# The operand buffer of a two-block transformer kernel, placed 32 bytes higher in SBUF

## The chip, the cores and the metric

The kernel runs on one core of one Trainium2 chip. The metric is the device time of one execution in microseconds (us); the kernel before took 1439.92 us as the median of 3 runs.

## The reference, cut to what matters

Two transformer blocks run one after the other on 256 tokens of width 1024, in float32. Nearly all of the work is products of normalised activations with weight matrices:

```python
def conformer_conv(h, ...):  # h @ w_pw1, gate, 31-tap convolution, layernorm, silu, @ w_pw2
def fox_attention(h, w_q, w_o, k, v, c_bhs): ...      # 16 heads
def memory_cross_attention(h, mem_n, ...): ...        # 4 heads, twice
def sqrelu_mlp(h, w1, w2):
    return jnp.square(jax.nn.relu(h @ w1)) @ w2       # 1024 -> 4096 -> 1024, twice
def swiglu(x, w_gate, w_up, w_down):
    return (jax.nn.silu(x @ w_gate) * (x @ w_up)) @ w_down   # 1024 -> 2816 -> 1024, twice
def token_mixing(u, w_in, ...):                       # u @ w_in (5136 columns), two attentions, @ w_out
...
u = modulate(rmsnorm_2(h, norm_ff1[l]), sh1, sc1)     # mod = silu(c) @ w_ada + b_ada
```

## The kernel before, in words

**Tiles.** Activations lie transposed: 128 partitions hold 128 features, KT = 8 such tiles make up the width, and the T = 256 tokens run along the free axis. Most products are made in "split" form. A tensor is kept as a high part, rounded to the type that TensorE reads in one pass (fp32r), and a low part that holds the rest. ScalarE writes the high part and VectorE the low part, for weights (`wsplit`, lines 1176 and 1753) as for activations.

**Buffers.** `hA` is the operand buffer of the normalised tiles: per feature tile 2 x 256 elements, the high block and then the low block. `hM`, `hB` and `hid` have the same layout. `hM` and `hB` hold the operands of the output projections (`hB` also a second normalised operand), `hid` the hidden activations of the four feed-forward parts; they and others share one 64 KB region behind the fixed buffers. `raw` receives weights by DMA, 1 MB a chunk in a ring of 4; `wsplit` is the ring of split weights.

**The two inner forms.** A pair (`block_cols`, lines 477 and 479) multiplies one 128 x 128 weight tile with both blocks of the operand at once (512 columns) and then the low weights with the high block (256 columns):

```python
        def tile_of(hl):
            return lambda kt: hl[:, kt, :].rearrange("p (s t) -> p s t", s=2)
        def block_cols(dst, w, lo_w, h, start, stop):
            nc.tensor.matmul(dst.rearrange("p (s t) -> p s t", s=2), w, h, ...)         # L477
            return nc.tensor.matmul(dst[:, 0:T], lo_w, h[:, 0, :], ...)                 # L479
```

In a pair the weights are the stationary operand, loaded ahead of each matmul (the rows of PEld), and the activations stream. A triple does the same as three matmuls of 256 columns: lines 536 to 538 (`whole_tile`, used for the last tiles of a residual and for the branch products), and 565 to 568 in the output projection of the first attention. In lines 516 to 518 (`split_values`, the values of the second memory attention), and in the pairs 636 and 640 (products that give rows: the value projections and part of the input projection), it is the other way round: `hA` is stationary and `wsplit` streams. Line 498 multiplies unsplit float32 tiles, some of them from `pw1_h`, which lies where `hA` lies.

**Order.** The stages follow one another on all engines by semaphores: pw1 and the memory projections in unsplit form (to about 155 us), memv1, pw2, memq0, memo0, up0, down0, the first attention, memq1, memo1, up1, down1, gu1, dn1, the input projections with the second attentions, branch, out, gu2, dn2. `hA` streams in memq, up, gu, the key projections of the first attention and most of the input projections; `hid` in down and dn. Beside this VectorE makes the modulation vector from `w_ada` in steps of 256 KB (line 2142, buffer `ada_w`, loaded on SP's queue), at listed chunks of down0, the first attention, down1, gu1, dn1, the input projections and gu2.

**Placement.** One function hands out bytes of a partition from a running cursor:

```python
        cursor = [-(-nc.sbuf_base // 32) * 32]
        def place(name, shape, dt=F32, at=None):
            size = int(np.prod(shape[1:])) * (2 if dt == BF16 else 4)
            if at is None:
                at = cursor[0]
                cursor[0] += -(-size // 32) * 32
            return nc.alloc_sbuf_tensor_at(name, shape, dt, offset=at)
```

Of the kernel before, what the change touches and what calls it, by code (L numbers as in the profile page):

```python
# [236 lines left out]
def program(nc, dram, out):  # L237
    ctx = ExitStack()
    with ctx:
# [9 lines that stand above are left out]
# [2 lines left out]
        wsplit = place("wsplit", [P, RING, 2, KT * 256], F32R)  # L251
        x = place("x", [P, KT, T])

        rel_rows = place("rel_rows", [P, G_HEADS, SKEW], at=cursor[0])
        hA_at = cursor[0]
        hA = place("hA", [P, KT, 2 * T], F32R)
        tsum = place("tsum", [P, 2, 2, T])
        aux = place("aux", [P, 2, 2, T])
        lowp = place("lowp", [P, 2, T])
# [2455 lines left out]
```

How the kernel before makes its waits and increments, by code:

```python
        @block.sync  # L401
# [5 lines left out]
            def load(st, c, known):  # L407
                slot = (st.base + known) % RING
                n = st.ring + known - RING
                if n >= 0:
                    prev = next(s for s in PLAN if s.ring <= n < s.ring + s.chunks)
                    sp.wait_ge(S("native_done" if prev.native else "w_lo"), c + (st.ring - RING - prev.ring + prev.base + 1))
                sp.dma_start(raw[:, slot, 0:st.elems], dram[st.name][c]).then_inc(raw_loaded[slot], 16)
# [12 lines left out]
            def ada_load(m):  # L427
                for half in range(2):
                    if m:
                        sp.wait_ge(S("ada_step"), 2 * (m - 1) + half + 1)
                    else:
                        sp.wait_ge(S("cond_silu"), 1)
                    sp.dma_start(ada_w[:, half, :], dram["ada"][m, half]).then_inc(ada_loaded[half], 16)
# [11 lines left out]
                    continue  # L446
                groups(sp, st.chunks, lambda c, known: load(st, c, known), begun=RING if st.ring == 0 else 0,
                       lead=RING if st.ring == 0 else 0)
            for p in range(PAIRS):
                sp.wait_ge(S("final_ready"), p + 1)
                sp.dma_start(out[:, 2 * p:2 * p + 2, :], x[:, 2 * p:2 * p + 2, :]).then_inc(S("stored"), 16)
            sp.wait_ge(S("stored"), 16 * PAIRS)
# [4 lines left out]
            def weights_ready(st, c):  # L458
                pe.wait_ge(S("w_hi"), c + (st.base + 1))
                pe.wait_ge(S("w_lo"), c + (st.base + 1))
```

## Time and profile before

| | us |
|---|---|
| median of 3 runs | 1439.92 |
| the 3 runs | 1438.95, 1439.92, 1442.92 |
| span of the profiled execution, first to last instruction | 1437.8 |
| TensorE matmuls busy | 1411.5 (98%) |
| VectorE busy | 1111.5 (77%) |
| ScalarE busy | 690.4 (48%) |
| DMA | 279.31 MB, mean 194 GB/s |

The profiled execution is given by its span; what a run takes beyond it is 2.1 us by the median. The profile has a time of its own only as that span. A busy TensorE is not yet a TensorE at full rate, since matmuls are pipelined and their ends are modelled: how fast it works is read from the distance between the starts of consecutive matmuls in the timeline. The chain of waits then tells in which stretches TensorE's rate sets the end, and in which another engine does.

### The profile page before, as it was taken

The page shows a single profiled execution, that of the slowest core. Times are in us where ns is not written, and L with a number is a line of the kernel's source. Part 1 is how long each engine was busy: PE and PEld are TensorE (multiplying, and loading weights), DVE is VectorE, ACT ScalarE, POOL GpSimd, SP SyncE. Part 2 cuts the span into 40 slices and gives each one's busy share as a digit, 9 for nine tenths or more (in the row PEclk, how much of TensorE's full clock was granted, in tenths as well). Part 3 has the DMA queues.
Part 4 walks back from the last instruction along what each step waited for, and adds up shares of the span by engine and source line. Part 5 has one row for each costly group of instructions (what it writes and reads, how often), then busy time and mean ns, then how long its engine had stood idle before and what let it go on. Part 6 is the DMA issues. An engine that isn't in the chain of part 4 may idle for free.

```text
span 1437.8 us, 21872 instructions
## 1 busy us (share of the span) xinstructions
PE 1411.5 (98%) x8580; PEld 1243.6 (86%) x8580; DVE 1111.5 (77%) x1660; ACT 690.4 (48%) x899; POOL 33.1 (2%) x21
## 2 busy tenths in 40 slices
PE   7999999999999999999999999999999999999997
PEld 6878998888889888888888988888988889888887
DVE  3799876698767887758887779997578678798664
ACT  2221664455434654645563355553454447555442
POOL 0000000000000000000000000000024100000000
PEclk9999999999999999999999999999999999999999
DMA  7444663355686456525558747757553436475451
GB/s 265 144 167 153 251 214 123 118 186 208 236 292 207 169 188 219 183 94 182 191 204 279 268 179 273 272 188 260 203 204 135 169 103 226 159 273 205 135 179 66
DMA packets 60150, 279.31 MB, mean 194 GB/s; under 512 B 6590, under 2 KB 8063, under 8 KB 35232
## 3 DMA queue, kind: packets, MB, share of 16 engines
q1 hardware_dynamic: 56248, 270.69, 53.7%
q10 hardware_dynamic: 3816, 7.45, 1.5%
q8 instruction: 58, 0.95, 0.3%
q14 instruction: 28, 0.23, 0.0%
HBM read 273.89 MB, written 4.19 MB: 193 GB/s over the span
## 4 chain that ended last, share of the span: by engine, by line
PE 84%; DVE 8%; DMA 5%; ACT 1%; issue 1%; DVEq 0%; SPq 0%; ACTq 0%
PE acc L477 34%; PE acc L479 17%; PE acc L498 10%; DMA ada_w<-in_ada 5%; PE acc L536 3%; PE acc L538 3%; PE acc L537 3%; DVE wsplit L1753 2%; PE acc L636 2%; PE stat L721 2%; DVE ada_w L2142 2%; PE acc L640 1%; PE turned L741 1%; PE stat L833 1%; PE score L1054 1%
## 5 line engine op out<-in xcount | busy, mean ns | idle before, releaser
L477 PE MATMUL acc<-hA,wsplit 128*128 128x512 f32 x1664 | 589.9, 399 | 4.4 <-DVE tsum L1767 1.7
L1176 ACT ACTIVATE wsplit<-raw 128x2048 fp32r<-128x2048 f32 (+3 forms) x214 | 381.2, 1783 | 195.3 <-PE acc L479 145.1
L1753 DVE TENSOR_TENSOR wsplit<-raw,wsplit 128x2048 fp32r<-128x2048 f32 (+3 forms) x214 | 455.1, 2130 | 16.4 <-ACT wsplit L1176 16.4
L479 PE MATMUL acc<-hA,wsplit 128*128 128x256 f32 x1664 | 463.9, 279 | 0.0
L477 PEld LDWEIGHTS acc<-hA,wsplit 128*128 128x128 f32 x1664 | 312.3, 188 | 81.6 <-issue 4.1
L479 PEld LDWEIGHTS acc<-hA,wsplit 128*128 128x128 f32 x1664 | 313.4, 188 | 0.4
L477 PE MATMUL acc<-hid,wsplit 128*128 128x512 f32 x648 | 224.9, 390 | 0.0
L479 PE MATMUL acc<-hid,wsplit 128*128 128x256 f32 x648 | 182.7, 282 | 0.0
L1186 ACT ACTIVATE lowp<-acc 128x512 f32<-128x512 f32 (+1 forms) x118 | 69.0, 585 | 202.8 <-PE acc L479 174.9
L477 PEld LDWEIGHTS acc<-hid,wsplit 128*128 128x128 f32 x648 | 121.6, 188 | 25.6
L479 PEld LDWEIGHTS acc<-hid,wsplit 128*128 128x128 f32 x648 | 122.5, 189 | 0.0
L2178 DVE SCALAR_TENSOR_TENSOR conv<-upad,taps,conv 128x256 f32<-128x256 f32 x240 | 98.2, 474 | 0.8
L2142 DVE CUSTOM_DVE_ANT_0 ada_w<-ada_w,cact,cols 128x512 f32<-128x512 f32 x72 | 55.0, 763 | 39.7 <-DMA ada_w<-in_ada 38.9
L2142 DVE CUSTOM_DVE_ANT_0 ada_w<-ada_w,cact,mod 128x512 f32<-128x512 f32 x72 | 54.9, 762 | 14.3 <-DMA ada_w<-in_ada 4.4
L536 PE MATMUL acc<-hid,wsplit 128*128 128x256 f32 x216 | 61.0, 282 | 0.0
L537 PE MATMUL acc<-hid,wsplit 128*128 128x256 f32 x216 | 60.3, 279 | 0.0
L538 PE MATMUL acc<-hid,wsplit 128*128 128x256 f32 x216 | 60.3, 279 | 0.0
L1763 DVE TENSOR_TENSOR tsum<-acc,lowp 128x512 f32<-128x512 f32 x40 | 27.6, 690 | 39.3 <-ACT lowp L1186 39.1
L498 PE MATMUL acc<-mem_h,raw 128*128 128x256 f32 x256 | 56.5, 380 | 0.0
L498 PEld LDWEIGHTS acc<-mem_h,raw 128*128 128x128 f32 x256 | 48.4, 190 | 8.7 <-issue 2.3
L498 PE MATMUL acc<-pw_h,raw 128*128 128x256 f32 x256 | 55.7, 379 | 0.0
L498 PEld LDWEIGHTS acc<-pw_h,raw 128*128 128x128 f32 x256 | 48.6, 190 | 6.6
(315 smaller groups left out, 2051.6 us busy)
## 6 DMA issues: line engine op xcount, KB each, us to landing
raw<-in_gu SPq DMA_DIRECT2D x44, 1024.0 KB, 4.9
ada_w<-in_ada SPq DMA_DIRECT2D x144, 256.0 KB, 4.8
raw<-in_up SPq DMA_DIRECT2D x32, 1024.0 KB, 4.9
raw<-in_down SPq DMA_DIRECT2D x32, 1024.0 KB, 5.0
raw<-in_dn SPq DMA_DIRECT2D x32, 704.0 KB, 4.1
raw<-in_pw SPq DMA_DIRECT2D x12, 1024.0 KB, 8.1
raw<-in_memk SPq DMA_DIRECT2D x8, 1024.0 KB, 4.8
raw<-in_memv SPq DMA_DIRECT2D x8, 1024.0 KB, 5.3
```

Of the source, the lines that this page charges most:

```text
L477: nc.tensor.matmul(dst.rearrange("p (s t) -> p s t", s=2), w, h, start=start, stop=False, skip_group_check=True)
L479: return nc.tensor.matmul(dst[:, 0:T], lo_w, h[:, 0, :], start=False, stop=stop, skip_group_check=True)
L498: mm = nc.tensor.matmul(acc[:, par, j, 0:T], lhs, rhs, start=kt == 0, stop=kt == KT - 1)
L536: nc.tensor.matmul(dst, w, h[:, 0, :], start=start, stop=False, skip_group_check=True)
L537: nc.tensor.matmul(dst, w, h[:, 1, :], start=False, stop=False, skip_group_check=True)
L538: return nc.tensor.matmul(dst, lo_w, h[:, 0, :], start=False, stop=stop, skip_group_check=True)
L636: nc.tensor.matmul(dst.rearrange("p (s n) -> p s n", s=2), h(kt)[:, 0, tt * P:(tt + 1) * P], w[:, :, kt * n:(kt + 1) * n], start=kt == 0, ...
L1176: nc.scalar.activation(wsplit[:, slot, 0, 0:elems_of(n)], raw[:, slot, 0:elems_of(n)], ACT.Copy).then_inc(S("w_hi"), 1)
L1186: last = nc.scalar.activation(lowp[:, :, 0:width], acc[:, par, :, width:2 * width], ACT.Copy)
L1753: V.tensor_tensor(wsplit[:, slot, 1, 0:e], raw[:, slot, 0:e], wsplit[:, slot, 0, 0:e].bitcast(F32), ALU.subtract).then_inc(S("w_lo"), 1)
L2142: V.tensor_tensor_reduce(w, w, cact[:, half * HALF:(half + 1) * HALF], 1.0, mod[:, m:m + 1] if half else col("ada_b", m), ALU.mult, ALU.ad ...
L2178: ins = V.scalar_tensor_tensor(out=conv[:, kt, :], in0=u, scalar=w, in1=conv[:, kt, :], op0=ALU.mult, op1=ALU.add)
```

## The change

The cursor is moved by 32 bytes ahead of `hA`, and by another 32 bytes behind it.

```diff
         x = place("x", [P, KT, T])
 
+        cursor[0] += 32
         rel_rows = place("rel_rows", [P, G_HEADS, SKEW], at=cursor[0])
         hA_at = cursor[0]
         hA = place("hA", [P, KT, 2 * T], F32R)
+        cursor[0] += 32
         tsum = place("tsum", [P, 2, 2, T])
```

All engines issue the same instructions in the same order on the same shapes. What differs is the byte offset of operands in their partition, as the built program has them:

| buffer | before | after | remainder by 64 | remainder by 128 | remainder by 256 |
|---|---|---|---|---|---|
| `raw` | 16512 | 16512 | 0 | 0 | 128 |
| `wsplit` | 49280 | 49280 | 0 | 0 | 128 |
| `x` | 114816 | 114816 | 0 | 0 | 128 |
| `hA`, `pw1_h`, `gain_sq`, `rel_rows` | 123008 | 123040 | 0, then 32 | 0, then 32 | 128, then 160 |
| `tsum` (and `aux`, `lowp`, `rstd`, `var`, `cols`, `mod`) | 139392 | 139456 | 0 | 0, then 64 | 128, then 192 |
| `ada_w` (and `cact`, `ones`, the masks, `small`) | 159648 | 159712 | 32 | 32, then 96 | 160, then 224 |
| `hid`, `hM`, `hB` | 163744 | 163808 | 32 | 32, then 96 | 160, then 224 |
| `fo`, `gl` | 204704 | 204768 | 32 | 32, then 96 | 160, then 224 |
| `mo` | 180128 | 180192 | 32 | 32, then 96 | 160, then 224 |

The tiles inside `hA`, `hM`, `hB` and `hid` lie 2048 bytes apart, the weight tiles inside `wsplit` 512 bytes, so that every tile has its buffer's remainder.

## Rows read from the trace of the kernel before

**Rows 1.** The page: busy time, the granted clock in 40 slices, the chain by engine.
```profile
PE 1411.5 (98%) x8580; PEld 1243.6 (86%) x8580; DVE 1111.5 (77%) x1660; ACT 690.4 (48%) x899; POOL 33.1 (2%) x21
...
PEclk9999999999999999999999999999999999999999
...
PE 84%; DVE 8%; DMA 5%; ACT 1%; issue 1%; DVEq 0%; SPq 0%; ACTq 0%
```
**Rows 2.** Groups of PE, by form: line, tiles, shape, count | busy us, mean ns | idle.
```profile
L477 PE MATMUL acc<-hA,wsplit 128*128 128x512 f32 x1664 | 589.9, 399 | 4.4 <-DVE tsum L1767 1.7 <-DVE x L1838 1.2 <-DVE hA L1969 0.8
L479 PE MATMUL acc<-hA,wsplit 128*128 128x256 f32 x1664 | 463.9, 279 | 0.0
L477 PE MATMUL acc<-hid,wsplit 128*128 128x512 f32 x648 | 224.9, 390 | 0.0
L479 PE MATMUL acc<-hid,wsplit 128*128 128x256 f32 x648 | 182.7, 282 | 0.0
...
L477 PE MATMUL acc<-hM,wsplit 128*128 128x512 f32 x144 | 50.5, 393 | 0.0
```
**Rows 3.** Timeline of PE in dn2, `hid`: start us, length; first and last of 28 L477.
```profile
1389.63 0.39 PE L477 MATMUL acc<-hid,wsplit 128*128 128x512 f32 x1
...
1398.99 0.39 PE L477 MATMUL acc<-hid,wsplit 128*128 128x512 f32 x1
```
**Rows 4.** Timeline of PE in gu2, `hA`: first and last of 26 L477.
```profile
1309.86 0.40 PE L477 MATMUL acc<-hA,wsplit 128*128 128x512 f32 x1
...
1318.69 0.40 PE L477 MATMUL acc<-hA,wsplit 128*128 128x512 f32 x1
```
**Rows 5.** Timeline of PE in up0, `hA`: first and last of 27 L477.
```profile
299.66 0.39 PE L477 MATMUL acc<-hA,wsplit 128*128 128x512 f32 x1
...
308.68 0.39 PE L477 MATMUL acc<-hA,wsplit 128*128 128x512 f32 x1
```
**Rows 6.** Chain of waits in gu1: start us, us, what.
```profile
849.31 0.69 DVE tsum L1767
...
852.90 4.88 DMA ada_w<-in_ada
...
948.14 0.50 PE acc L477
```
**Rows 7.** Chain of waits in gu2.
```profile
1249.91 0.61 ACT lowp L1186
...
1254.19 4.93 DMA ada_w<-in_ada
...
1298.09 0.51 PE acc L477
```
**Rows 8.** Timeline of PE in the input projections, `hA`: first and last of 10 L477.
```profile
1073.90 0.40 PE L477 MATMUL acc<-hA,wsplit 128*128 128x512 f32 x1
...
1077.09 0.40 PE L477 MATMUL acc<-hA,wsplit 128*128 128x512 f32 x1
```
**Rows 9.** Timeline of PE in memv1, `hA` stationary: first and last of 18 L516.
```profile
171.74 0.28 PE L516 MATMUL acc<-wsplit,hA 128*128 128x256 f32 x1
...
177.86 0.28 PE L516 MATMUL acc<-wsplit,hA 128*128 128x256 f32 x1
```
**Rows 10.** Timeline of PE in down0, triples of `hid`: first and last of 21 L536.
```profile
445.92 0.28 PE L536 MATMUL acc<-hid,wsplit 128*128 128x256 f32 x1
...
452.92 0.28 PE L536 MATMUL acc<-hid,wsplit 128*128 128x256 f32 x1
```
**Rows 11.** Timeline of PE, row products, `hA` stationary: first and last of 14 L636.
```profile
1096.61 0.40 PE L636 MATMUL acc<-wsplit,hA 128*128 128x512 f32 x1
...
1101.20 0.40 PE L636 MATMUL acc<-wsplit,hA 128*128 128x512 f32 x1
```
**Rows 12.** Groups of DVE, by form: the low block written into `hA` and into `hB`.
```profile
L1824 DVE TENSOR_TENSOR hA<-tsum,hA 128x512 fp32r<-128x512 f32 x13 | 8.9, 686 | 3.2 <-ACT hA L1260 3.2
...
L1982 DVE TENSOR_TENSOR hB<-tsum,hB 128x512 fp32r<-128x512 f32 x4 | 2.7, 687 | 0.1
```
**Rows 13.** Timeline of PE behind down0, bf16 matmuls of 256 columns.
```profile
457.76 4.09 PE L741 MATMUL turned<-mask_bf,ident_bf 128*128 128x256 bf16 x36
```

## The prediction

> **What bounds the kernel now.** First the page's busy times, the clock and the chain [rows 1]: TensorE is busy 98% of the span, the granted clock shows 9 in all 40 slices (its upper level, 2.4 GHz, throughout), and 84% of the chain is PE. So the end is set, for the most part, by how fast TensorE works through its matmuls. No instruction moves, so no wait is added or removed by the program. The only thing that can change is how long an access to SBUF takes at another address. The question is thus whether any duration in the trace depends on the place of an operand.
>
> Next the groups by form [rows 2]. The same line 477, on the same shape and with the same weights buffer, has a mean of 399 ns where `hA` streams and 390 ns where `hid` streams; line 479 has 279 against 282. Matmul ends are modelled, so I go to the starts in the timeline. In dn2, where `hid` streams, 28 starts of L477 span 1398.99 - 1389.63 = 9.36 us, that is 27 periods of 346.7 ns [rows 3]. In gu2, where `hA` streams, 26 starts span 8.83 us, 25 periods of 353.2 ns [rows 4]. A pair with `hA` is there 6.5 ns longer. But `hA` isn't always slower: in up0 27 starts span 9.02 us, 26 periods of 346.9 ns [rows 5].
>
> Counted from start to start over the whole trace, all pairs of `hid`, `hM` and `hB` that wait for nothing keep one period of about 346.7 ns, from the third pair after any wait on. Pairs of `hA` fall into one of several repeating patterns, of 347, 353 or 360 ns, keep it for many chunks, and leave it at a stall. The only property that separates the two kinds of buffer and that the change touches is the address: `hA` begins at a multiple of 64 (as `wsplit` does), the others 32 bytes past one. After the change `hA` has the remainder that `hid` had, by 64, by 128 and by 256. I read the rows so: which patterns exist depends on the phase between the stream and the weights, and at 32 there is one alone, the fast one.
>
> **The change, part by part.** *The operand streams from its new place (pairs).* I price each stage by its own surplus over 346.7 ns, and count it only where the chain runs through PE.
> - up0, up1 and the first part of gu1: no surplus [rows 5], nothing to gain.
> - gu1 up to 948.14: from 849.31 to there the chain is VectorE's in-order queue and the loads of `ada_w`, such as the 4.88 us at 852.90 [rows 6]. A faster TensorE only waits longer for it, so the surplus of some 0.6 us late in this stretch goes into that wait. Behind it 3 of the 22 chunks are left: 48 pairs x 6.5 ns = 0.3 us.
> - gu2: from 1249.91 to 1298.09 the chain is again VectorE and `ada_w` [rows 7]; 136 pairs x 6.5 ns = 0.9 us would be lost in the wait at its end. Before it 24 pairs give 0.15 us; behind it 12 chunks, 192 pairs x 6.5 ns = 1.25 us.
> - Input projections: 256 pairs of `hA`, chunks between 347 and 354 ns; the chunk shown has 3.19 us for 9 periods, 354.4 ns [rows 8]. I take half of that surplus, 3.5 ns, for all: 0.9 us. The 64 pairs of the key projections likewise: 0.2 us.
> - memq0, memq1: steady pairs at 347, nothing.
>
> Sum: 0.3 + 0.15 + 1.25 + 0.9 + 0.2 = 2.8 us.
>
> *The operand is stationary.* In memv1 `hA` is loaded as weights: 18 starts of L516 span 6.12 us, 360.0 ns a triple [rows 9], while a triple of `hid` takes 7.00 us / 20 = 350.0 ns [rows 10]. For 64 triples that is 0.6 us. The row products have 4.59 us / 13 = 353.1 ns in the chunk shown [rows 11]; half of that surplus over 128 pairs is 0.4 us. No row shows a stationary operand at 32 beside a stream at 0, so this is bounded by 0 and 1.0 us; I take half, 0.5 us, since it is the same two streams with their roles exchanged.
>
> *Branch.* 64 triples of `gl`, `mo` and `hA` follow one another there, so that the pattern of one may carry into the next; bounded by 0 and 64 x 10 ns = 0.6 us; I take 0.3.
>
> *Everything else.* VectorE's writes into the buffer: 686 ns at 0, 687 ns at 32 in `hB` [rows 12], so nothing. The buffers behind keep their remainder by 64; I price them at nothing and put the doubt into a rival.
>
> Sum: 2.8 + 0.5 + 0.3 = **3.6 us less**. The span of 1437.8 us becomes 1434.2, and with the 2.1 us that the median has above that span the forecast is 1439.9 - 3.6 = **1436.3 us**. The bounds of the priced terms are 2.8 and 4.4 us; if the chain misleads in gu1 and gu2 and TensorE's surplus counts there too, another 1.5: 5.9 us, 1434.0.
>
> **The rivals.** *The place doesn't matter: 1439.9 us.* For it: `hA` reached 346.9 ns at its old place in up0 [rows 5], so the place alone doesn't make it slow; `hA` differs from `hid` also by lying some 40 KB lower, and a pattern could come from where the last stall fell. Against it: `hid`, `hM` and `hB` start anew many times, also straight after `hA`, and always end in the same period.
>
> The Trainium skill speaks for this rival. Its page "SBUF — State Buffer", section "SBUF: two separate sides", has it that TensorE and ScalarE have ports of their own and never wait for anyone. Its page "TensorE: Matmul & The Clock Gate", section "Step-by-step: what each phase is for", gives the stream and the weights independent read ports. And that page's section "Back-to-back issue gap" has N / 2.4 + 2.5 ns between warm matmuls, 215.8 + 109.2 = 325 ns for a pair, wherever it lies. By these rules the change would be worth 0. The bf16 matmuls of 256 columns agree, with 36 of them in 4.09 us [rows 13]; the pairs don't, since 346.7 is above 325, and 353.2 beside 346.7 on one shape isn't foreseen.
>
> *Slower: the buffers behind leave their good phase.* `hid`, `hM`, `hB` and `fo` go from remainder 32 to 96 by 128. If the pattern repeats at 128 bytes (or 256) and not at 64, then `hA` gains as above, but 904 pairs that now have one fast pattern could fall into one like that of gu2: 904 x 6.5 ns = 5.9 us, and their 344 triples into that of memv1: 344 x 10 ns = 3.4 us. down and dn lie on TensorE's part of the chain, so it counts in full: 1436.3 + 9.3 = 1445.6 us. It decides where the period is above 64. Nothing in the trace excludes it, since all tiles that stream in pairs lie at 0 or 32 by 128; for a shorter period speaks only that the smaller step is the simpler reading. *The same mechanism with the other sign*: at 96 the pairs could also find a shorter pattern than any seen; with the same size, 5.9 us, the time would be 1430.4.
>
> That the change doesn't do what it says is excluded: the built program has the new offsets.
>
> **How the numbers follow.** A measurement of this kernel can tell about 0.3%, 4.3 us, from no change: faster is below 1435.6, slower above 1444.2. Chances: forecast 0.61, no effect of the place 0.24, slower 0.09, the shorter pattern 0.06. The forecast's own spread (1434.0 to 1437.1, and about 1 us of scatter between medians) puts a third of its chance below 1435.6: 0.21, with the last case 0.27; slower 0.10, of which a little is scatter; the rest, 0.63, within 0.3%. The range for 8 in 10 goes from 1433.6, just below the strongest form of the forecast, to 1441.8, the no-change case with the scatter that the runs before show above their median; it leaves out most of the slower case and the shorter pattern.
>
> **What would show it.** Right: in gu2 the starts of L477 are 346.7 ns apart, and L477 and L479 of `hA` have means near 390 and 282 ns; memv1's triples are at 350; the waits ahead of 948 and 1298 us grow by about 0.6 and 0.9 us, with the loads of `ada_w` in the chain as before; down and dn keep 346.7. Wrong: gu2 still at 353 (the place doesn't matter), or `hid` at 353 or 360 (the period is above 64). If `hA`'s pairs are all at 346.7 but the span shrinks by less than 2.8 us, the step on the chain is at fault.

## The result, and the profile after

The changed kernel takes 1443.85 us (median of 12 runs, 1442.94 to 1444.49), the kernel before 1439.74 us in the runs beside it (1438.95 to 1442.92): ratio 1.0024, 95% interval 1.0017 to 1.0031. It is 4.1 us **slower**. I forecast 3.6 us less, so the sign was wrong, and the time lies above my range.

The page of the changed kernel, busy times and the chain by engine (lines below L256 carry numbers higher by 2 than before, so L477 is now L479):

```profile
PE 1415.1 (98%) x8580; PEld 1250.2 (87%) x8580; DVE 1111.4 (77%) x1660; ACT 690.4 (48%) x899; POOL 33.2 (2%) x21
...
PE 84%; DVE 8%; DMA 5%; ACT 1%; issue 1%; DVEq 0%; SPq 0%; ACTq 0%
```

Nothing has moved between engines: same shares as in [rows 1]. So the periods have to tell. First gu2, where `hA` streams, first and last of 27 starts of L479 in the timeline of PE:

```profile
1308.65 0.39 PE L479 MATMUL acc<-hA,wsplit 128*128 128x512 f32 x1
...
1317.67 0.39 PE L479 MATMUL acc<-hA,wsplit 128*128 128x512 f32 x1
```

9.02 us for 26 periods: 346.9 ns, where [rows 4] had 353.2. That is as forecast. (The views give starts to 0.01 us, so a period read over 26 of them is good to about 0.4 ns: 346.5, 346.7 and 346.9 are the same.) Then dn2, where `hid` streams, first and last of 27 starts:

```profile
1393.85 0.39 PE L479 MATMUL acc<-hid,wsplit 128*128 128x512 f32 x1
...
1402.95 0.39 PE L479 MATMUL acc<-hid,wsplit 128*128 128x512 f32 x1
```

9.10 us for 26 periods: 350.0 ns, where [rows 3] had 346.7. This buffer moved by 64 bytes, and I had priced that at nothing. The triples of `hid` in down0, first and last of 23 starts of L538 (L536 before):

```profile
446.72 0.28 PE L538 MATMUL acc<-hid,wsplit 128*128 128x256 f32 x1
...
454.64 0.28 PE L538 MATMUL acc<-hid,wsplit 128*128 128x256 f32 x1
```

7.92 us for 22 periods: 360.0 ns, where [rows 10] had 350.0. And memv1, `hA` stationary, first and last of 18 starts of L518 (L516 before):

```profile
171.81 0.28 PE L518 MATMUL acc<-wsplit,hA 128*128 128x256 f32 x1
...
177.85 0.28 PE L518 MATMUL acc<-wsplit,hA 128*128 128x256 f32 x1
```

6.04 us / 17 = 355.3 ns, where [rows 9] had 360.0: half of the possible gain, which would have ended at 350.0.

**A ledger.** The two kernels issue the same 8580 matmuls in the same order, so each start of one can be set against the same start of the other. The difference grows or shrinks stage by stage; added up over the traces:

| stages | what streams | change, us |
|---|---|---|
| start, up to pw1 | `aux` | +0.9 |
| down0, down1, dn1, dn2 | `hid` | +4.3 |
| pw2, memo0, memo1, outputs of the first attention | `hM`, `hB`, `fo` | +1.4 |
| branch, out | `gl`, `mo`, `hA`, then `hM` | +0.5 |
| memv1, memq, gu1, input projections, gu2 | mostly `hA` | -2.6 |
| end | | +4.5 |

The mean durations are treacherous here. For `hid` they were 390 and 282 ns in [rows 2] and are now:

```profile
L479 PE MATMUL acc<-hid,wsplit 128*128 128x512 f32 x648 | 227.1, 393 | 0.0
L481 PE MATMUL acc<-hid,wsplit 128*128 128x256 f32 x648 | 180.9, 279 | 0.0
```

393 + 279 is the same sum as 390 + 282, although the period of the pair grew by 3.3 ns. Ends of matmuls are modelled in the profile; only the starts showed it.

The 0.9 us at the start can't be put down to the change. The first matmul of pw1 begins at 13.37 us in the profile of before, at 14.27 in the one after, and between 13.56 and 14.60 in the profiles of the eight kernels below, with a different number of the first statistics matmuls (L721, 16 of them) 426 ns apart and most of the others 216. Before has the earliest of the ten. Without this start the spans of the two profiles differ by 3.6 us. There is one profile for each kernel, so whether the start scatters from run to run of one kernel isn't shown; the medians include it.

### The profile page after: what moved, and what is told of

Same layout as the page of the kernel before. It is cut to its first block, busy times and chain, and to the rows that moved or that the text cites. A ratio compares the mean times of both kernels' runs of the same rounds, so it can differ in the third digit from the quotient of the medians.

```text
span 1442.4 us, 21872 instructions
## 1 busy us (share of the span) xinstructions
PE 1415.1 (98%) x8580; PEld 1250.2 (87%) x8580; DVE 1111.4 (77%) x1660; ACT 690.4 (48%) x899; POOL 33.2 (2%) x21
## 4 chain that ended last, share of the span: by engine, by line
PE 84%; DVE 8%; DMA 5%; ACT 1%; issue 1%; DVEq 0%; SPq 0%; ACTq 0%
PE acc L479 34%; PE acc L481 17%; PE acc L500 10%; DMA ada_w<-in_ada 5%; PE acc L538 3%; PE acc L540 3%; PE acc L539 3%; DVE wsplit L1755 2%; PE acc L638 2%; PE stat L723 2%; DVE ada_w L2144 2%; PE acc L642 1%; PE turned L743 1%; PE stat L835 1%; PE score L1056 1%
## 5 line engine op out<-in xcount | busy, mean ns | idle before, releaser
L479 PE MATMUL acc<-hA,wsplit 128*128 128x512 f32 x1664 | 585.9, 394 | 5.1 <-DVE tsum L1769 2.4
L481 PE MATMUL acc<-hA,wsplit 128*128 128x256 f32 x1664 | 469.0, 282 | 0.0
L479 PEld LDWEIGHTS acc<-hA,wsplit 128*128 128x128 f32 x1664 | 312.4, 188 | 74.7 <-DVE tsum L1769 4.6
L479 PE MATMUL acc<-hid,wsplit 128*128 128x512 f32 x648 | 227.1, 393 | 0.0
L479 PEld LDWEIGHTS acc<-hid,wsplit 128*128 128x128 f32 x648 | 121.4, 187 | 29.1
L538 PE MATMUL acc<-hid,wsplit 128*128 128x256 f32 x216 | 61.8, 286 | 0.0
```

Source lines behind the costliest of these rows:

```text
L481: return nc.tensor.matmul(dst[:, 0:T], lo_w, h[:, 0, :], start=False, stop=stop, skip_group_check=True)
L538: nc.tensor.matmul(dst, w, h[:, 0, :], start=start, stop=False, skip_group_check=True)
```

## The experiments

Three theories stood against each other. **A**: what counts is the phase of the streamed operand against the stationary one (for a pair, the distance from `wsplit`), and it repeats not before 128 bytes. **B**: the absolute place of the streamed operand counts. **C**: the loss comes from `hA`, or from the small buffers between. All remainders below are by 128.

### Only hA moves

```diff
+        mod = place("mod", [P, N_MOD * KT])
         rel_rows = place("rel_rows", [P, G_HEADS, SKEW], at=cursor[0])
...
-        mod = place("mod", [P, N_MOD * KT])
```

> Only hA moves to remainder 32 (by 64, 128 and 256): mod, 288 bytes, is placed ahead of hA in place of behind it, so hid, hM, hB, fo, ada_w and ones keep their old offsets; tsum, aux, lowp, rstd, var and cols go from 0 to 32. Theory A (the phase of the streamed operand against the weights, repeating at 128 bytes: 32 good, 0 mixed, 96 bad): pairs of hA at 346.8 ns, pairs of hid stay at 346.7, triples of hid at 350.0, memv1's triples near 355; the time is that of before less the 2.1 us that the changed kernel won in memv1, gu1, gu2 and the projections, 1437.6 us. Theory B (the absolute place of the streamed operand by 128) expects the same. Theory C (the buffers tsum to cols, or a stretch that scatters, make the loss, not hid's place): hid's pairs go to 350 here too, and the time is 1441 or more.

1436.97 us beside 1439.93: ratio 0.9979, interval 0.9970 to 0.9988. The timeline of PE in gu2 and dn2, first and last of 27 starts each:

```profile
1304.71 0.39 PE L477 MATMUL acc<-hA,wsplit 128*128 128x512 f32 x1
...
1313.72 0.39 PE L477 MATMUL acc<-hA,wsplit 128*128 128x512 f32 x1
...
1387.90 0.39 PE L477 MATMUL acc<-hid,wsplit 128*128 128x512 f32 x1
...
1396.92 0.39 PE L477 MATMUL acc<-hid,wsplit 128*128 128x512 f32 x1
```

9.01 and 9.02 us for 26 periods: 346.5 and 346.9 ns, both in the fast pattern. Triples of `hid` kept 350.0 (counted over all), memv1 had 355.1. So the half of my forecast that concerned `hA` holds, with -3.0 us for the -3.6 that I had worked out. Theory C falls for `hA`, and for `tsum` to `cols` at 32, which moved here too; at 64, where the changed kernel has them, they lie in the run with everything moved below, and cost nothing there. This version beats both kernels. How its gain divides over the stages is less sure than its sum: in its one profile gu1 took 0.95 us more than before, behind longer waits for VectorE, and gu2 2.28 us less.

### Only the buffers behind move

```diff
         hA = place("hA", [P, KT, 2 * T], F32R)
+        cursor[0] += 64
```

> hA stays at 0, everything behind it moves by 64 (hid from 32 to 96 by 128). Theories A and B: pairs of hid, hM and hB at 350.0 ns, triples at 360, hA's pairs as before (347 to 360, mean 349.6); the changed kernel lost 5.5 us in these stages, so 1439.7 + 5.5 = 1445.2 us. Rival (the loss comes from hA's move): hid at 346.7 and 1439.7 us.

1446.32 us, ratio 1.0039 (1.0025 to 1.0053): 6.4 us slower. dn2, first and last of 26 starts:

```profile
1393.93 0.39 PE L478 MATMUL acc<-hid,wsplit 128*128 128x512 f32 x1
...
1402.67 0.39 PE L478 MATMUL acc<-hid,wsplit 128*128 128x512 f32 x1
```

8.74 us / 25 = 349.6 ns (350.0 over all pairs of `hid` that wait for nothing), the triples at 359.9. The result splits in two: -3.0 us from `hA` and +6.4 from the rest add up to 3.4, and 4.1 were measured for both together, which agrees within the intervals.

### Everything moves by 64

```diff
+        cursor[0] += 64
         raw = place("raw", [P, RING, KT * 256])
```

> Everything from raw on moves by 64: weights at 64, hA at 64, hid at 96 by 128, all distances between buffers as before. Theory A (the phase against the weights): all periods as before, hid's pairs at 346.7, its triples at 350, 1439.7 us. Theory B (the absolute place): hid's pairs at 350.0 and triples at 360 as in the changed kernel; hA at 64 is unknown to it; 1444 to 1447 us.

1440.38 us, ratio 1.0001 (0.9992 to 1.0010): no difference. `hid` lies at 96 as in the changed kernel, but its distance to the weights is still 32. dn2, first and last of 27 starts:

```profile
1389.68 0.39 PE L478 MATMUL acc<-hid,wsplit 128*128 128x512 f32 x1
...
1398.69 0.39 PE L478 MATMUL acc<-hid,wsplit 128*128 128x512 f32 x1
```

9.01 us / 26 = 346.5 ns. Theory B falls: the same absolute place, 163808 in both, gave 350.0 in the changed kernel and gives 346.7 here. Not every period was as before, though: `hA`, at distance 0 as before, had 353.2 ns throughout gu1, where its mean was 349.2. Most of gu1 is covered by VectorE and `ada_w` [rows 6], so this hardly shows in the time.

### The weights move under an operand that stays

```diff
+        mod = place("mod", [P, N_MOD * KT])
         wsplit = place("wsplit", [P, RING, 2, KT * 256], F32R)
...
-        mod = place("mod", [P, N_MOD * KT])
```

> mod, 288 bytes, is placed ahead of wsplit: wsplit, x, hA and tsum to cols move by 288, from 0 to 32 by 128; cact, ones, ada_w, hid, hM, hB, fo, gl and mo don't move at all. So hid's distance to the weights becomes 0 by 128, hA's stays 0. Theory A (the phase between stream and weights, by 128): although neither hid nor any instruction on it moves, its pairs take up the mixed patterns that hA has at distance 0 (347 to 360 ns, mean about 349.6), its triples 357 to 360, hA as before; 904 x 2.9 ns + 344 x 8 ns = 5.4 us more than before, about 1445 us. Theory B (the absolute place of the stream): hid as before at 346.7 and 350, hA good at 32: about 1437 us.

1445.63 us, ratio 1.0036 (1.0022 to 1.0049). `hid` didn't move by a byte; the weights did. The timeline of PE in down0 and in dn2, first and last of 27 starts each:

```profile
374.85 0.40 PE L477 MATMUL acc<-hid,wsplit 128*128 128x512 f32 x1
...
383.87 0.40 PE L477 MATMUL acc<-hid,wsplit 128*128 128x512 f32 x1
...
1394.71 0.40 PE L477 MATMUL acc<-hid,wsplit 128*128 128x512 f32 x1
...
1403.89 0.40 PE L477 MATMUL acc<-hid,wsplit 128*128 128x512 f32 x1
```

346.9 ns in down0 (and so in down1), 9.18 us / 26 = 353.1 ns in dn2 (and so in dn1): `hid` now has the two patterns that `hA` had in [rows 4, 5], on the same code, and its triples take 359.7 ns, as those with `hA` in memv1 did [rows 9]. This is the clearest of the runs: a stream becomes slower because the other stream moved.

One rival is left: VectorE and ScalarE write `wsplit` while TensorE reads it, and it could be their writes that get in the way. The trace of the changed kernel speaks against it. In dn2 the 56 pairs that start while VectorE writes `wsplit` have a mean period of 350.0 ns, the 34 that start while ScalarE alone writes it 350.1, and the 40 others 349.9.

### hid at a distance of 64

```diff
         hA = place("hA", [P, KT, 2 * T], F32R)
+        cursor[0] += 32
```

> hA stays at 0, everything behind it moves by 32: hid is at 64 by 128, 0 by 64. If the pattern repeated at 64 bytes, hid would now behave as hA does at 0: pairs between 347 and 360 ns, mean 349.6, triples 357 to 360, some 5 us slower than before, 1445 us. If it repeats at 128 bytes (theory A), 64 is a phase of its own that no run has shown; bounded by the best and the worst period seen, 346.7 and 360 ns for pairs, 350 and 360 for triples: 1439.7 to 1455 us.

1449.96 us, ratio 1.0064 (1.0050 to 1.0078). In dn2 27 starts span

```profile
1397.68 0.40 PE L478 MATMUL acc<-hid,wsplit 128*128 128x512 f32 x1
...
1406.86 0.40 PE L478 MATMUL acc<-hid,wsplit 128*128 128x512 f32 x1
```

9.18 us / 26 = 353.1 ns, and so in all four stages of `hid`; triples at 353.4. A repetition at 64 bytes would have made this like distance 0, with triples at 359.7: that is excluded. A surprise came with it. `hA` hadn't moved, yet in up0, first and last of 26 starts, its pairs went as follows:

```profile
299.90 0.40 PE L478 MATMUL acc<-hA,wsplit 128*128 128x512 f32 x1
...
308.73 0.40 PE L478 MATMUL acc<-hA,wsplit 128*128 128x512 f32 x1
```

8.83 us for 25 periods, 353.2 ns in place of 346.9 [rows 5], which cost 1.7 us in up0 and again in up1. At distance 0 there are two patterns, and the distance alone doesn't say which one a stage falls into. So the 10 us of this run aren't `hid`'s alone. Distance 64 has more than one pattern as well: `hM` had 349.0 ns in pw2 and out and 353.4 in memo0, and 12 triples of `fo` took 340 ns each, six of them between the first and the last of these 7 starts of L566:

```profile
563.38 0.28 PE L566 MATMUL acc<-fo,wsplit 128*128 128x256 f32 x1
...
565.42 0.28 PE L566 MATMUL acc<-fo,wsplit 128*128 128x256 f32 x1
```

2.04 us / 6 = 340 ns, the shortest triple of all runs.

### hA at 64, and both at 96

```diff
+        cursor[0] += 64
         rel_rows = place("rel_rows", [P, G_HEADS, SKEW], at=cursor[0])
```

> hA at 64, hid at 96 by 128, weights at 0. Theory A expects of hA at 64 what hid had there: pairs at 353.3 ns in every stage, up0 and up1 too; hid's pairs at 350.0 and triples at 360 as in the changed kernel. 1664 pairs x 3.7 ns above the mean that hA had at 0, less the sixth of them that VectorE and ada_w cover: some 5 us above the kernel with the same place of hid and hA at 0 (1446.3), 1451 us. If every buffer had a phase table of its own, hA's pairs could lie anywhere from 346.7 to 360.

1451.23 us, ratio 1.0078 (1.0065 to 1.0092); `hA`'s pairs at 353.0 over all that wait for nothing. In up0, first and last of 27 starts:

```profile
301.78 0.40 PE L478 MATMUL acc<-hA,wsplit 128*128 128x512 f32 x1
...
310.96 0.40 PE L478 MATMUL acc<-hA,wsplit 128*128 128x512 f32 x1
```

9.18 us / 26 = 353.1 ns, as `hid` has at 64. The second has `mod` ahead of `hA` as in the first experiment, and 64 bytes more:

```diff
+        cursor[0] += 64
+        mod = place("mod", [P, N_MOD * KT])
         rel_rows = place("rel_rows", [P, G_HEADS, SKEW], at=cursor[0])
...
-        mod = place("mod", [P, N_MOD * KT])
```

> hA and hid both at 96 by 128, weights at 0. Theory A: all pairs at 350.0 ns, those of hA in up0, up1 and gu too, where they were at 346.7 or 353 before; triples at 360; the same tables for hA as for hid. Against the kernel with hid at 96 and hA at 0 (1446.3 us, hA's pairs at a mean of 348.9) some 1 us more, about 1447 us. Rival (each buffer has a table of its own, set by its place at large): hA's pairs differ from hid's.

1446.67 us, ratio 1.0048 (1.0032 to 1.0063); pairs of `hA` at 350.1 and of `hid` at 350.0, triples at 359.9. Where they stream, both buffers follow one table. The row products, where `hA` is stationary and the weights stream, are now at a distance, stream less stationary, of 0 - 96, that is 32 by 128. Their timeline, first and last of 12 starts:

```profile
1104.85 0.39 PE L637 MATMUL acc<-wsplit,hA 128*128 128x512 f32 x1
...
1108.67 0.39 PE L637 MATMUL acc<-wsplit,hA 128*128 128x512 f32 x1
```

3.82 us / 11 = 347 ns, and so in all four chunks of the input projections, where before three had 353 [rows 11] and one 347. With `hA` at 32 they are at distance 96. In the changed kernel one of the four chunks then had 347 ns; the second, first and last of 13 starts once it is steady:

```profile
1109.26 0.40 PE L638 MATMUL acc<-wsplit,hA 128*128 128x512 f32 x1
...
1113.50 0.40 PE L638 MATMUL acc<-wsplit,hA 128*128 128x512 f32 x1
```

4.24 us / 12 = 353.3 ns, as in the two behind it; in the run with only `hA` moved all four had 353. So the sign of the distance matters, as it does for `hid`, with 346.7 ns at 32 and 350.0 at 96, which is -32. But the row products at 96 don't have `hid`'s 350.0, and memv1's triples, also at distance 32 now, don't have the 350.0 that `hid` had at 32. First and last of 18 starts of L517:

```profile
171.55 0.28 PE L517 MATMUL acc<-wsplit,hA 128*128 128x256 f32 x1
...
177.60 0.28 PE L517 MATMUL acc<-wsplit,hA 128*128 128x256 f32 x1
```

6.05 us / 17 = 355.9 ns. The table below is therefore one of buffers that stream against `wsplit` as the stationary operand.

### hA at 48

```diff
-        hA = place("hA", [P, KT, 2 * T], F32R)
+        hA = place("hA", [P, KT * 2 * T + 8], F32R)[:, 4:4 + KT * 2 * T].rearrange("p (k t) -> p k t", k=KT)
```

with `mod` ahead of it as in the first experiment.

> hA at 48 by 128 (a tensor 32 bytes wider at 32, used from its 16th byte on), hid at 64, weights at 0. hid costs by its place what it cost at 64 before: 904 x 6.6 + 344 x 3.4 ns = 7.1 us on top of 1437. If the pattern depends on blocks of 32 bytes, hA at 48 behaves as at 32: pairs at 346.8 and 1444 us. If it depends on the place more finely, hA's pairs take another period, bounded by 346.7 and 360 ns, up to 1444 + 1400 x 13 ns = 1462 us.

1443.52 us, ratio 1.0026 (1.0017 to 1.0035). The time is as expected for 32-byte blocks, but not for that reason. `hA` in up0 and gu2, first and last of 27 starts each:

```profile
301.83 0.40 PE L477 MATMUL acc<-hA,wsplit 128*128 128x512 f32 x1
...
310.93 0.40 PE L477 MATMUL acc<-hA,wsplit 128*128 128x512 f32 x1
...
1311.94 0.40 PE L477 MATMUL acc<-hA,wsplit 128*128 128x512 f32 x1
...
1320.95 0.40 PE L477 MATMUL acc<-hA,wsplit 128*128 128x512 f32 x1
```

9.10 and 9.01 us for 26 periods: 350.0 in up0, 346.5 in gu2, so 16 bytes do make a difference. And `hid`, at 64 again, had 348.8 ns in down0, down1 and dn2 (9.07 us / 26) where the earlier run with 64 had 353.1, and 353.2 in dn1. So at 64 `hid`, too, has more than one pattern. `hid` gained about what `hA` lost, which is luck and not an effect of 32-byte blocks. What picks the pattern stays open.

The table that the runs give for a buffer that streams, as the distance from the stationary to the streamed operand (streamed less stationary) by 128:

| distance | period of a pair, ns | period of a triple, ns | seen with |
|---|---|---|---|
| 0 | 347 or 353 | 359.7 | `hA` before, `hid` with the weights moved |
| 32 | 346.7 to 347.5 in every stage | 350.0 | `hid` before, `hA` after |
| 48 | 347 or 350 | not read | `hA` |
| 64 | 353 or 349 | 353.4, 12 of `fo` at 340 | `hid`, `hA`, `hM`, `fo` |
| 96 | 350.0 | 359.9 | `hid` after, both at 96 |

With `hA` stationary and `wsplit` streaming:

| distance by 128 | by 256 | period of a pair (row products), ns | period of a triple (memv1), ns |
|---|---|---|---|
| 0 | 0 | 347 or 353 | 360.0 |
| 96 (`hA` at 32) | 224 | 347 or 353 | 355.0 |
| 64 (`hA` at 64) | 192 | 353.3 | 353.3, the first five 340 |
| 32 (`hA` at 96) | 160 | 346.7 | 356.1 |

Whether it repeats at 128 or at 256 can't be told: all distances of the first table are below 128 by 256 too, those of the second, but for 0, above. So whether the two tables differ because the roles are exchanged or because the period is 256 stays open as well. A period above 256 isn't needed for 32: `hA` after lies at 32 by 512 and `hid` before at 288, and both had 346.7.

## Why the prediction was wrong

1. *The place of the operand sets the pattern of the pairs.* Right: I read it as a phase between the stream and the weights, and the runs with everything moved and with the weights moved show just that. That there is one pattern alone at 32 held too. But a pattern of 360 ns for pairs, which the prediction names, isn't there: in the trace of before, distances of 361 ns stand between two of 350 in the 353 pattern of gu2, and the 347 of up0 is 343 and 350 by turns. The Trainium skill ("SBUF — State Buffer", section "SBUF: two separate sides") says that TensorE never waits on anyone. It says so of contention between engines; taken as the prediction took it, to mean that the place of an operand doesn't matter, it isn't borne out: 346.7 against 353.1 ns for `hid` at one and the same place differ from it, and the measurement decides. The prediction's 325 ns for a pair is an estimate by a formula that the Trainium skill ("TensorE: Matmul & The Clock Gate", section "Back-to-back issue gap") gives for isolated matmuls and not for streams with weight loads between, so that 346.7 lies above it says nothing about the place.
2. *hA's terms.* Right in kind, slightly large in size. Alone they gave -3.0 us (-4.3 to -1.7 by the interval), for -3.6. `hA`'s pairs came to 346.8 over all. The chain was read rightly. In gu2 the wait ahead of L477 (L479 after) at the end of VectorE's stretch [rows 7] grew from 0.17 to 0.84 us (in brackets). Before:

```profile
1298.09 0.51 PE L477 MATMUL acc<-hA,wsplit 128*128 128x512 f32 x1 [0.17 <-DVE tsum L1767]
```

after:

```profile
1303.00 0.50 PE L479 MATMUL acc<-hA,wsplit 128*128 128x512 f32 x1 [0.84 <-DVE tsum L1769]
```

And gu1 gained only the 0.3 us behind 948 [rows 6] in the changed kernel: up to there it took as long as before. Its surplus didn't go into the wait ahead of 948, as forecast, which stayed at 1.5 us, but mostly into shorter ones at the starts of three chunks before it. memv1 gave 0.3 of the 0.6 us that was possible, as I took it. The row products gave nothing: exchanged roles turn the distance round, to 96, which I hadn't thought of. The branch gave its 0.3 us with `hA` alone; in the change, branch and out lost 0.5, because `gl`, `mo` and `hM` went to 96.
3. *"The buffers behind keep their remainder by 64; I price them at nothing"*. **This is the step that failed.** What mattered was the distance to the weights by 128 (or 256), which went from 32 to 96, and it cost 6.4 us. The table of offsets showed it, and I had put it into the rival with a chance of 0.09 on the ground that a smaller step is the simpler reading. That was no evidence: no buffer in the trace of before separates 64 from 128.
4. *The rival's price.* The result lies 1.8 us below the rival's 1445.6: its mechanism was right, and one of its two terms too large. It put 9.3 us on top of the forecast; measured were 6.4 (the run with the buffers behind alone), in two terms. Triples: 344 x 10 ns, exactly as priced (350.0 to 359.9). Pairs: 904 x 3.3 ns = 3.0 us, for the 904 x 6.5 = 5.9 us that I took from gu2's pattern; at 96 the pattern is a third one, milder than that of gu2. 3.4 + 3.0 = 6.4, what the run measured; that they meet so closely is in part luck, since the branch, slower by 0.3 us in that run's trace, isn't in the sum.

## What to carry to other kernels

When two streams of one engine are read side by side, compare their distance by a larger power of two than the step that the edit happens to keep: an edit that restores the remainder by 64 can still move everything behind it. And when a trace shows that a buffer at some place is good, move the other buffer to that place and leave the good one where it is, here by putting a 288-byte tensor ahead of the operand in place of 32 + 32 bytes of padding. Read such effects from start to start over some 25 periods, not from mean durations, whose modelled ends hid a change of 3.3 ns in the sum.

## What the runs showed of the hardware

TensorE's rate on fp32r operands depends on where the streamed operand lies against the stationary one. With `wsplit` stationary, a pair takes 346.7 ns at a distance of 32 bytes by 128, 350.0 at 96 and 353 at 64, and a triple 350.0 at 32, 353.4 at 64 and 360 at 96. At 0, 48 and 64 the same code at the same distance can settle in more than one pattern and keep it for whole stages: in the run with `hid` at 64, `hA`, which hadn't moved, went from 346.9 to 353.2 ns in up0. What picks the pattern wasn't found. The unsplit float32 matmuls of line 498 don't follow this: from start to start they keep 215.8 ns on average in the traces before and after, though `pw1_h` moved with `hA`.
